# Second block: projections of x times the norm weight, with 1/rms applied to their products, and gate/up two slices ahead

## The chip, the cores and the metric

One core of one Trainium2 chip runs the whole program. The metric is the device time of one execution in microseconds; lower is better.

## What is computed

One sequence of 256 tokens with 1024 features passes two blocks. The first (two layers of a mixer with a state space scan, and a mixture of experts) isn't touched, but for the cut of one weight tile per layer. The second has four layers, each a mixer and an FFN, both behind an RMS norm:

```python
def rms_norm_2(x, g):
    y = xf * lax.rsqrt(jnp.mean(xf * xf, axis=-1, keepdims=True) + EPS)
    return (y * g.astype(F32)).astype(x.dtype)

def swiglu(h, w_gate_up, w_down):
    g, u = jnp.split(h @ w_gate_up, 2, axis=-1)
    return (jax.nn.silu(g) * u) @ w_down

for i in range(4):
    h = rms_norm_2(x, mix_norm_g[i])
    # i = 0, 3: forgetting_attention (q, k, v and 16 forget logits from h @ w_in)
    # i = 1: s5_layer (u = h @ w_in, scan, gelu, glu); i = 2: multiscale_pool
    x = x + mix
    x = x + swiglu(rms_norm_2(x, ffn_norm_g[i]), ffn_w_gate_up[i], ffn_w_down[i])
return rms_norm_2(x, final_norm_g)
```

The norm's factor 1/rms belongs to a token, so it commutes with a projection over features.

## The kernel before

x stands in SBUF with features on partitions, as 8 chunks of 128 features by 256 tokens. Every matmul of a projection is made of three (`mm3`, L655): weight and activation are both split into a rounded "high" part and the rest, "low", and high by high, high by low, low by high are added up in PSUM. Weights come as tiles of 1024 features by 256 columns (1 MB) into a ring of four (`ring`), loaded by SP's queue once `tile_free` says that the tile four before was used. For tile t ACT writes high (`make_high`, L1204, 128x2048 elements) into one of two buffers, so only after tile t-2 is free; then DVE and POOL each subtract one half for low (`make_low`, L362), and PE waits for both in `low_ready` (L353). The down weights of the FFN go the same way in tiles of 128 by 1024 (`make_down_high` L1214, `make_down_low` L373), with `down_free` in place of `tile_free`; down high (d) waits until d-2 was used. Each engine works through its own program in order.

A norm goes: ACT squares x by pairs of chunks (`squares`, L1239), PE sums them over partitions with 8 matmuls against 1/1024 (`mean_square`, L694), ACT takes the root (`root`, L1245), DVE the reciprocal and then, by chunk, x * gain / rms (`scale`, L1615), ACT its high part (`split_high`, L1249), DVE its low (L1626). PE starts a projection when chunk 0 is there and waits for each further one (`ready`).

A projection (`project`, L703) is a list of groups of 24 matmuls, two groups per weight tile, that write to PSUM banks in turn; an eviction frees a bank. In fox (layers 0 and 3, PE L1006, ACT L1469, DVE L2047) the forget logits come first in a tile of their own (`foxf`), then 24 groups of `foxin` (8 of V, 8 of Q, 8 of K, all evicted by ACT), then attention over 16 heads, then 8 groups of `foxout`, whose results DVE adds to x (`residual`, L1838). s5 (layer 1) has 8 groups of `s5in`, a scan loop, and 16 of `glu`. Layer 2 pools on DVE and needs the whole normed h.

An FFN has 22 slices of 128 hidden features (PE L964, ACT L1450, DVE L2011, POOL L502). `gate_up(j)` is 48 matmuls into bank 4 + j % 2 (gate in one half, up in the other), `down(j)` 24 into banks 0 to 3, which collect all slices. The order on PE is gate_up(j+1), down(j). Written out, the order of the other engines for slice j is

```python
# ACT: wait tile_free; silu(gate) -> gact; make_high(tile j+2); make_down_high(j+1)
# DVE: wait gact; hraw = gact * up (PSUM); hid high; hid low; make_low(tile j+2); make_down_low(j+1)
# POOL: make_low(tile j+2); make_down_low(j+1)
```

where tile j+2 for the last two slices is the first or second of the next stage. In FFN 0 DVE also computes the s5 matrices behind slices 1 to 3 (`s5_matrices`, L2139). After down(21) DVE adds the banks to x (`add_sum`, L2033).

## Time and profile before

| what | value |
|---|---|
| runs | 2779.86, 2789.84, 2791.86 us |
| median | 2789.84 us |
| profiled execution: span | 2783.9 us |
| profiled execution: own time beside the span | none given by the page |
| mean granted TensorE clock | 0.894 of full |
| PE / PEld busy | 2328.6 / 1960.5 us (84% / 70%) |
| DVE / ACT / POOL busy | 1625.2 / 1104.4 / 1323.9 us (58% / 40% / 48%) |
| second block | from about 1290 us to the end |

A row of a timeline gives start and length in us, engine, line, operation and what it writes and reads; in square brackets the idle time before and the engine and line that ended it. PE is the matmul stream, PEld its weight loads. The tiles have the program's names: `high` and `ring_halves` are a weight's high and low, `dhigh` and `dring_halves` the down weight's, `ssdb_halves` and `HT_halves` the activation's, `border` the hidden slice, `bank` PSUM, `wide` holds the squares.

### The profile page before, as it was taken

Reading aid. Unit: us, or ns where it says so; the run is one execution under the profiler, and the core shown is the slowest. Engines: PE = TensorE matmul, PEld = TensorE weight load, DVE = VectorE, ACT = ScalarE, POOL = GpSimd, SP = SyncE. Lnnn points to the kernel's source line nnn. Section 1 sums busy time; section 2 is a strip of 40 time slices with the busy share of each in tenths; the row PEclk is TensorE's granted clock in tenths of the full one; section 3 lists DMA queues with packets and bytes.
Section 4 is the critical chain, followed back from the end, with each engine's and each line's share of the span. In section 5 each row is a group of like instructions: output and inputs, shape, how many; then the busy total and the mean of one; then the engine's idle time right before and its main releaser. Section 6 shows DMA issues by size and latency. Waiting matters only on the chain.

```text
span 2783.9 us, 41385 instructions
## 1 busy us (share of the span) xinstructions
PE 2328.6 (84%) x15250; PEld 1960.5 (70%) x15250; DVE 1625.2 (58%) x2522; ACT 1104.4 (40%) x1581; POOL 1323.9 (48%) x744
## 2 busy tenths in 40 slices
PE   5998777788498767785999997768999799999998
PEld 2864545677385466674868995325899699887998
DVE  3488464477558545674247555996555755523654
ACT  3222533466433435764434442001443344444443
POOL 2320132588442336882654552874565256441553
PEclk7995888899797888997989998668999899999999
DMA  5258602699326037883405441001455244342442
GB/s 228 91 202 322 217 15 91 228 341 344 144 96 252 1 112 268 321 296 133 171 24 199 186 172 71 0 0 52 165 192 189 91 181 182 135 152 91 152 181 91
DMA packets 93047, 443.73 MB, mean 159 GB/s; under 512 B 9088, under 2 KB 25600, under 8 KB 56704
## 3 DMA queue, kind: packets, MB, share of 16 engines
q1 hardware_dynamic: 79104, 390.10, 38.6%
q0 software_dynamic: 8496, 31.99, 3.0%
q10 hardware_dynamic: 5328, 20.04, 1.8%
q8 instruction: 77, 1.26, 0.2%
q14 instruction: 42, 0.34, 0.0%
HBM read 401.20 MB, written 40.89 MB: 159 GB/s over the span
## 4 chain that ended last, share of the span: by engine, by line
PE 40%; DVE 5%; POOL 3%; ACT 2%; DVEq 2%; POOLq 1%; issue 1%; DMA 0%; ACTq 0%
PE bank L657 11%; PE bank L658 11%; PE bank L659 11%; POOL ring_halves L371 2%; PE bank L699 2%; ACT high L1212 1%; PE bank L1123 1%; POOLq L593 1%; DVEq L2179 1%; PE bank L1061 1%; DVE HT L1633 1%; POOLq L598 1%; PE bank L1038 1%; DVE rstd L1618 1%; PE bank L1051 1%
## 5 line engine op out<-in xcount | busy, mean ns | idle before, releaser
L371 POOL TENSOR_TENSOR ring_halves<-ring,high 128x1024 fp32r<-128x1024 f32 (+1 forms) x230 | 814.2, 3541 | 953.9 <-ACT high L1212 953.9
L657 PE MATMUL bank<-ssdb_halves,high 128*128 128x256 f32 (+1 forms) x2080 | 619.6, 298 | 65.8 <-DVE HT_halves L1627 34.8
L658 PE MATMUL bank<-HT_halves,high 128*128 128x256 f32 (+1 forms) x2096 | 627.4, 299 | 0.0
L659 PE MATMUL bank<-ssdb_halves,ring_halves 128*128 128x256 f32 (+1 forms) x2080 | 615.5, 296 | 0.0
L1212 ACT CAST high<-ring 128x2048 fp32r<-128x2048 f32 x230 | 438.0, 1906 | 89.7 <-PE bank L659 89.7
L657 PEld LDWEIGHTS bank<-ssdb_halves,high 128*128 128x128 f32 x2080 | 400.8, 193 | 90.5 <-issue 61.2
L371 DVE TENSOR_TENSOR ring_halves<-ring,high 128x1024 fp32r<-128x1024 f32 x200 | 279.5, 1398 | 248.0 <-ACT high L1212 247.9
L658 PEld LDWEIGHTS bank<-HT_halves,high 128*128 128x128 f32 x2096 | 402.6, 192 | 8.9
L659 PEld LDWEIGHTS bank<-ssdb_halves,ring_halves 128*128 128x128 f32 x2080 | 398.4, 192 | 9.6
L378 DVE TENSOR_TENSOR dring_halves<-dring,dhigh 128x512 fp32r<-128x512 f32 x152 | 309.6, 2037 | 53.1 <-ACT dhigh L1218 53.0
L378 POOL TENSOR_TENSOR dring_halves<-dring,dhigh 128x512 fp32r<-128x512 f32 x152 | 264.5, 1740 | 80.7 <-ACT dhigh L1218 80.6
L657 PE MATMUL bank<-border_halves,dhigh 128*128 128x256 f32 x704 | 197.5, 281 | 0.0
L659 PE MATMUL bank<-border_halves,dring_halves 128*128 128x256 f32 x704 | 197.3, 280 | 0.0
L658 PE MATMUL bank<-border_halves,dhigh 128*128 128x256 f32 x704 | 197.3, 280 | 0.0
L1218 ACT CAST dhigh<-dring 128x1024 fp32r<-128x1024 f32 x152 | 160.8, 1058 | 54.2 <-PE bank L659 54.1
L659 PE MATMUL bank<-high,HT_halves 128*128 128x256 f32 x640 | 182.0, 284 | 0.0
L1456 ACT ACTIVATE border<-bank 128x256 f32<-128x256 f32 x88 | 33.8, 384 | 365.0 <-PE bank L659 365.0
L657 PE MATMUL bank<-high,HT_halves 128*128 128x256 f32 x512 | 156.8, 306 | 18.0 <-POOL ring_halves L371 11.0
L2017 DVE TENSOR_TENSOR border<-border,bank 128x256 f32<-128x256 f32 x88 | 37.1, 422 | 213.9 <-ACT border L1456 213.1
L1123 PE MATMUL bank<-wide,zs_b 128*32 128x256 f32 x256 | 96.7, 547 | 62.5 <-DVE wide L2190 62.5
L658 PE MATMUL bank<-ring_halves,HT_halves 128*128 128x256 f32 x512 | 145.5, 284 | 0.0
L657 PEld LDWEIGHTS bank<-border_halves,dhigh 128*128 128x128 f32 x704 | 132.6, 188 | 0.1
(415 smaller groups left out, 4603.3 us busy)
## 6 DMA issues: line engine op xcount, KB each, us to landing
ring<-in_ffn SPq DMA_DIRECT2D x88, 1024.0 KB, 5.4
ring<-in_moe SPq DMA_DIRECT2D x64, 1024.0 KB, 7.3
ring<-in_ada SPq DMA_DIRECT2D x48, 1024.0 KB, 6.9
dring<-in_ffn_down SPq DMA_DIRECT2D x88, 512.0 KB, 3.6
dring<-in_moe_down SPq DMA_DIRECT2D x64, 512.0 KB, 4.6
ring<-in_foxin SPq DMA_DIRECT2D x24, 1024.0 KB, 4.8
ring<-in_win SPq DMA_DIRECT2D x22, 1024.0 KB, 4.8
zs_b<-x_slots POOLq DMA_DIRECT2D x32, 512.0 KB, 8.8
```

The costliest lines, as they stand in the source:

```text
L371: eng.tensor_tensor(low, w, h, ALU.subtract).then_inc(sem(f"low_{engine}"), 1)
L378: eng.tensor_tensor(low, w, h, ALU.subtract).then_inc(sem(f"down_low_{engine}"), 1)
L593: pool.drain()
L657: mm(o, a[0], b[0], start=first, stop=last and bool(kw), **kw)
L658: mm(o, a[0], b[1], start=False, stop=last and bool(kw), **kw)
L659: return mm(o, a[1], b[0], start=False, stop=last, **kw)
L699: i = mm(ps[7][:, 0:tok.stop - tok.start], k("mean1024"), sq[:, c, tok], start=c == 0, stop=c == KC - 1)
L1123: i = mm(y, cT[:, part, j, :], z, start=False, stop=n == 3, skip_group_check=True, tile_position=(0, q))
L1212: nc.scalar.copy(r(high[c % HIGH][:]), ring[t % RING][:]).then_inc(sem("high"), 1)
L1218: nc.scalar.copy(r(dhigh[d % HIGH][:]), dring[d % RING][:]).then_inc(sem("down_high"), 1)
L1456: act_fn(gact[:, j % 2, :], ps[4 + j % 2][:, 0:T], ACT.Silu).then_inc(sem("gate_act"), 1)
L2017: tt(hraw, gact[:, j % 2, :], ps[4 + j % 2][:, T:2 * T], ALU.mult)
```

## The change

For every projection of the second block behind a norm (all but pooling), ACT now writes the high part of x * gain straight from x, chunk by chunk as x gets ready (`x_high`), and the squares with it; DVE writes the low part (`x_low`), called from inside the loops that add to x. DVE adds the squares of the 8 chunks up (`square_sum`), so that PE's mean is one matmul (`sum_squares`), placed behind the first groups; root and reciprocal follow (`inv_root`). 1/rms then multiplies the products: DVE evicts Q, K and s5's u with it, ACT V with a column of it that PE turns, DVE the forget logits; in the FFN DVE multiplies gate and up by it from PSUM into `gu` (SBUF), which silu and the product read. The first groups run side by side, chunk by chunk (`first`, `gate_up_first`). In the FFN PE's order is gate_up(j+2), down(j). Forget logits' softplus moves behind group 12. Weight tiles outside the FFNs and experts are cut at three quarters for DVE, one for POOL. `F2r` is a second place for the low part, so that x_low can write while foxout and glu still read `H2r`.

The core of the diff:

```diff
+            CUT.append(0 if _n[0] not in WITH_DVE else TILE // 2 if _n[0] in IN_SLICES else 3 * TILE // 4)
...
-            cut = TILE // 2 if shared(c) else 0
+            cut = CUT[c]
...
+            def sum_squares(n):
+
+                pe.wait_ge(*at("row_stats", ("sum", n)))
+                mm(ps[7][:, 0:T], k("mean1024"), sq[:, 0, 0:T], start=True, stop=True).then_inc(*done("mean_square", n))
...
+                if first is not None:
+                    heads = [(n, j, lag, out_ap(ps[bank]), pairs(*low_ready(SPLIT_AT[n]))) for n, j, bank, lag, (out_ap, pairs) in first]
+                    for step in range(KC + max(h[2] for h in heads)):
+                        if step < KC:
+                            pe.wait_ge(*ready(step))
+                        for n, j, lag, o, pairs in heads:
+                            if 0 <= step - lag < KC:
+                                i = mm3(o, *next(pairs), step == lag, step - lag == KC - 1)
+                                if step - lag == KC - 1:
+                                    group_done(n, j, i)
+                    start = 1 + max(j for n, j, *_ in first if n == name)
...
+                    if j >= 2 or not isinstance(g, int):
+                        pe.wait_ge(sem("gu_scaled"), gu0 + j - 1 + RING * g)
...
+                def gate_up_first():
+
+                    wh, wl = low_ready(c0)
+                    for c in range(KC):
+                        pe.wait_ge(*ready(c))
+                        for m in range(2):
+                            a = slice(c * TCOLS + m * P, c * TCOLS + m * P + P)
+                            i = mm3(ps[4][:, m * T:m * T + T], (wh[:, a], wl[:, a]), (r(xh(c)), r(xl(c))),
+                                    c == 0 and m == 0, c == KC - 1, skip_group_check=True)
...
-                gate_up(0, 0, ready)
-                turns = (slices - 1) // RING
+                gate_up_first()
+                for b in range(4):
+                    mm(ps[b][:], zeros[:, 0:P], zeros, start=True, stop=True)
+                sum_squares(mean)
+                gate_up(1, 0)
+                turns = (slices - 2) // RING
                 with pe.Fori(0, turns) as g:
                     for j in range(RING):
-                        gate_up(j + 1, g)
+                        gate_up(j + 2, g)
                         down(j, g)
                 for j in range(turns * RING, slices):
-                    if j + 1 < slices:
-                        gate_up(j + 1, 0)
+                    if j + 2 < slices:
+                        gate_up(j + 2, 0)
                     down(j, 0)
...
+                def after(j):
+                    if j == 2:
+                        sum_squares(name)
+                    if j == 3:
+                        pe.wait_ge(*at("row_stats", ("rstd", name)))
+                        for b in range(TB):
+                            i = mm(ps[7][:, 300 + b:301 + b], rstd[0:1, b * P:b * P + P], one[0:1, 0:1], start=True, stop=True)
+                        i.then_inc(*done("mean_square", ("col", i_layer)))
+                    if j == 6:
+                        narrow_turned(("foxf", i_layer), 16, 7, 256, TB).then_inc(*done("f_raw", i_layer))
...
+                        [(("foxf", i_layer), 0, 5, 0, forget), (("foxin", i_layer), 0, 0, 0, groups[0])], after)
...
+                        lambda j: at("u_sb", j), [(("s5in", 1), j, j, 2 * j, groups[j]) for j in range(2)],
+                        lambda j: sum_squares(("s5",)) if j == 2 else None)
...
+            def x_high(n, c, gain, ready):
+
+                act.wait_ge(*ready(c))
+                act_fn(r(H2h[:, c, :]), XT2[:, c, :], ACT.Identity, scale=gain[:, c:c + 1]).then_inc(*done("norm_high", (n, c)))
+                if c % 2:
+                    act_fn(sq[:, c - 1:c + 1, 0:T], XT[:, c - 1:c + 1, 0:T], ACT.Square).then_inc(*done("squares", (n, c // 2)))
...
+            def swiglu(name, slices, n):
+                c0, d0, gu0 = SPLIT_AT[name], DOWN_AT[name], base("gu_scaled", name)
                 loop_base("gate_act", name, slices)

                 def one(j, g):
-                    act.wait_ge(sem("tile_free"), t0 + j + 1 + RING * g)
-                    act_fn(gact[:, j % 2, :], ps[4 + j % 2][:, 0:T], ACT.Silu).then_inc(sem("gate_act"), 1)
+                    act.wait_ge(sem("gu_scaled"), gu0 + j + 1 + RING * g)
+                    act_fn(gact[:, j % 2, :], gu[:, 0], ACT.Silu).then_inc(sem("gate_act"), 1)
                     make_high(c0 + j + 2, g)
                     if j + 1 < slices:
                         make_down_high(d0 + j + 1, g)

                 make_down_high(d0)
+                root(n, slice(0, T))
                 slices_loop(act, slices, one, 1 if d0 == 0 else 0)
...
+                root(("fox", i_layer), slice(0, T))
+                act.wait_ge(*at("row_stats", ("col", i_layer)))
+                for j in range(8):
                     act.wait_ge(*proj_at(("foxin", i_layer), j))
-                    bank = ps[j % 4]
-                    if j < 8:
-                        i = nc.scalar.copy(vtok[:, j % 2, TCOLS * (j // 2):TCOLS * (j // 2) + TCOLS], bank[:, 0:TCOLS])
-                    elif j < 16:
-                        i = nc.scalar.mul(Q2[:, j - 8, :], bank[:, 0:T], HD ** -0.5)
-                    else:
-                        i = nc.scalar.copy(K2[:, j - 16, :], bank[:, 0:T])
-                    i.then_inc(*done("fox_sb", (i_layer, j)))
+                    act_fn(vtok[:, j % 2, TCOLS * (j // 2):TCOLS * (j // 2) + TCOLS], ps[j % 4][:, 0:TCOLS], ACT.Identity,
+                           scale=r_col[:, j % 2:j % 2 + 1]).then_inc(*done("v_sb", (i_layer, j)))
                     tiles_after(("foxin", i_layer), j)
+                for j in range(9, 24, 2):
+                    tiles_after(("foxin", i_layer), j)
+                    if j == 11:
+                        softplus_log("f", i_layer, fx[:, 3, :, :], fx[:, 1, :, :])
...
+                root(("s5",), slice(0, T))
+                for j in range(1, KC, 2):
                     tiles_after(("s5in", 1), j)
...
                 for c in range(KC):
@@ -1527,6 +1584,9 @@
                         act.wait_ge(*at("res_dve", (("glu", 1), j - 2)))
                     act_fn(sig[:, j % 2, 0:T], ps[4 + (2 * j + 1) % 4][:, 0:T], ACT.Sigmoid).then_inc(*done("glu_gate", j))
                     tiles_after(("glu", 1), 2 * j + 1)
+                    if j:
+                        x_next(j - 1)
+                x_next(KC - 1)

             ada(0)
             root(("mix", 0), slice(0, 2 * T))
@@ -1564,21 +1624,27 @@
                 make_high(SPLIT_AT["foxf", 0] + a)
             for i_layer in range(4):
                 name = (("fox", 0), ("s5",), ("pool",), ("fox", 3))[i_layer]
-                squares(name, slice(0, T), lambda c: at("x_ready", (("ffn", i_layer - 1), c) if i_layer else ("first", c)))
-                root(name, slice(0, T))
-                if i_layer != 2:
-                    split_high(name, H2h, H2, None, 1)
+                x_ready = lambda c: at("x_ready", (("ffn", i_layer - 1), c) if i_layer else ("first", c))
+                if i_layer == 2:
+                    squares(name, slice(0, T), x_ready)
+                    root(name, slice(0, T))
+                else:
+                    for c in range(KC):
+                        x_high(name, c, v(f"mix_g{i_layer}"), x_ready)
                 last_res = (("foxout", 0), ("glu", 1), ("poolw", 2), ("foxout", 3))[i_layer]
+                x_next = lambda c: x_high(("ffn2", i_layer), c, v(f"ffn_g{i_layer}"), lambda c: at("res_dve", (last_res, c)))
                 if i_layer in (0, 3):
                     fox(i_layer)
-                    for a in range(HALF_D):
-                        tiles_after(last_res, 2 * a + 1)
+                    for c in range(KC):
+                        if c % 2:
+                            tiles_after(last_res, c)
+                        x_next(c)
...
+            def x_low(n, c, gain, to):
+
+                dve.wait_ge(*at("norm_high", (n, c)))
+                stt(r(to[:, c, :]), XT2[:, c, :], gain[:, c:c + 1], H2h[:, c, :], ALU.mult, ALU.subtract)\
+                    .then_inc(*done("normed", (n, c)))
+
+            def square_sum(n):
+
+                dve.wait_ge(*at("squares", (n, KC // 2 - 1)))
+                for a in (4, 2, 1):
+                    i = tt(sq[:, 0:a, 0:T], sq[:, 0:a, 0:T], sq[:, a:2 * a, 0:T], ALU.add)
+                    if a > 1:
+                        dve.drain()
+                i.then_inc(*done("row_stats", ("sum", n)))
+
+            def inv_root(n):
+
+                dve.wait_ge(*at("root", n))
+                nc.vector.reciprocal(rstd[:, 0:T], rms[:, 0:T]).then_inc(*done("row_stats", ("rstd", n)))
...
+                    if then is not None and j:
+                        then(j - 1)
+                    if then is not None and j == KC - 1:
+                        then(j)
                     if j % 2:
                         tiles(name, j // 2)
...
                 def one(j, g):
+                    dve.wait_ge(sem("tile_free"), t0 + j + 1 + RING * g)
+                    tt(gu, ps[4 + j % 2][:].rearrange("p (a b) -> p a b", a=2), rstd[:, 0:T].unsqueeze(1).to_broadcast([P, 2, T]),
+                       ALU.mult).then_inc(sem("gu_scaled"), 1)
+                    if c0 + j + 2 < len(SPLIT):
+                        make_low(dve, "dve", c0 + j + 2, g)
                     dve.wait_ge(sem("gate_act"), act0 + j + 1 + RING * g)
-                    tt(hraw, gact[:, j % 2, :], ps[4 + j % 2][:, T:2 * T], ALU.mult)
+                    tt(hraw, gact[:, j % 2, :], gu[:, 1], ALU.mult)
                     dve.drain()
+                    dve.wait_ge(sem("down_free"), d0 + j - 1 + RING * g)
                     nc.vector.tensor_copy(r(hid[:, j % 2, 0, :]), hraw)
                     dve.drain()
                     tt(r(hid[:, j % 2, 1, :]), hraw, hid[:, j % 2, 0, :], ALU.subtract).then_inc(sem("hidden"), 1)
-                    if c0 + j + 2 < len(SPLIT):
-                        make_low(dve, "dve", c0 + j + 2, g)
                     if j + 1 < slices:
                         make_down_low(dve, "dve", d0 + j + 1, g)
                     if between is not None and isinstance(g, int) and 1 <= j < RING:
                         between(j - 1)
                     dve.drain()

+                square_sum(n)
                 make_down_low(dve, "dve", d0)
+                inv_root(n)
...
+            def fox(i_layer, then):
+                name = ("foxin", i_layer)
+                square_sum(("fox", i_layer))
+                tiles(("foxf", i_layer))
+                inv_root(("fox", i_layer))
+                dve.wait_ge(*proj_at(("foxf", i_layer), 0))
+                tt(narrow_sb[0:16, 0:T], ps[5][0:16, 0:T], rstd[0:16, 0:T], ALU.mult).then_inc(*done("narrow_sb", ("foxf", i_layer)))
+                dve.wait_ge(*at("mean_square", ("col", i_layer)))
+                nc.vector.tensor_copy(r_col, ps[7][:, 300:300 + TB]).then_inc(*done("row_stats", ("col", i_layer)))
+                for j in range(24):
+                    if j >= 8:
+                        dve.wait_ge(*proj_at(name, j))
+                        if j < 16:
+                            i = stt(Q2[:, j - 8, :], ps[j % 4][:, 0:T], HD ** -0.5, rstd[:, 0:T], ALU.mult, ALU.mult)
+                        else:
+                            i = tt(K2[:, j - 16, :], ps[j % 4][:, 0:T], rstd[:, 0:T], ALU.mult)
+                        i.then_inc(*done("row_stats", ("qk", i_layer, j)))
+                    if j % 2:
+                        tiles(name, j // 2)
+                    if j == 12:
+                        forget(i_layer)
+                attend(i_layer)
+                residual(("foxout", i_layer), [0, 1, 2, 3], then=then)
...
+                square_sum(("s5",))
+                inv_root(("s5",))
+                for j in range(KC):
+                    dve.wait_ge(*proj_at(("s5in", 1), j))
+                    tt(Q2[:, j, :], ps[j % 4][:, 0:T], rstd[:, 0:T], ALU.mult).then_inc(*done("u_sb", j))
+                    if j % 2:
+                        tiles(("s5in", 1), j // 2)
```

## Rows read from the trace of the kernel before

**Rows 1.** The page: its first line, and the chain by engine.

```profile
span 2783.9 us, 41385 instructions
...
PE 40%; DVE 5%; POOL 3%; ACT 2%; DVEq 2%; POOLq 1%; issue 1%; DMA 0%; ACTq 0%
```

**Rows 2.** Windows, inside FFN 0: us; PE, PEld, DVE, ACT, POOL busy; clock; DMA.

```profile
1500.00:1670.00 170.00, 170.00 (x1443) 169.86 (x1441) 106.51 (x114) 69.92 (x65) 98.47 (x40) 1.00 0.49 181
```

**Rows 3.** Joints after fox 0 and FFN 0: chain in time; ACT timeline; one window.

```profile
1472.03 1.90 ACT high L1212
1474.51 5.42 PE bank L699 x16
...
1674.43 0.64 ACT wide L1242
...
1679.38 1.75 DVE rstd L1618
...
1500.80 1.05 ACT L1218 CAST dhigh<-dring 128x1024 fp32r<-128x1024 f32 x1 [0.66 <-PE bank L659]
...
1485.40:1488.80 3.40, 3.40 (x15) 3.12 (x15) 3.08 (x9) 2.26 (x5) 0.00 (x0) 0.51 0.02 5
```

**Rows 4.** Timelines of ACT, DVE, POOL, one FFN slice: start, us, operation [idle before].

```profile
1549.13 0.38 ACT L1456 ACTIVATE border<-bank 128x256 f32<-128x256 f32 x1 [4.60 <-PE bank L659]
1549.41 1.90 ACT L1212 CAST high<-ring 128x2048 fp32r<-128x2048 f32 x1
...
1549.55 0.42 DVE L2017 TENSOR_TENSOR border<-border,bank 128x256 f32<-128x256 f32 x1 [2.63 <-ACT border L1456]
...
1550.41 0.42 DVE L2021 TENSOR_TENSOR border_halves<-border,border_halves 128x256 fp32r<-128x256 f32 x1
1551.35 1.22 DVE L371 TENSOR_TENSOR ring_halves<-ring,high 128x1024 fp32r<-128x1024 f32 x1 [0.51 <-ACT high L1212]
1553.07 2.30 DVE L378 TENSOR_TENSOR dring_halves<-dring,dhigh 128x512 fp32r<-128x512 f32 x1 [0.49 <-ACT dhigh L1218]
...
1551.39 3.43 POOL L371 TENSOR_TENSOR ring_halves<-ring,high 128x1024 fp32r<-128x1024 f32 x1 [3.33 <-ACT high L1212]
```

**Rows 5.** One line's instructions over the run: ns min/median/max.

```profile
L371 POOL TENSOR_TENSOR ring_halves<-ring,high x230: 2354/3431/4852, 49.6 to 2748.3; 128x1024 fp32r<-128x1024 f32 x99, 128x2048 fp32r<-128x2048 f32 x16
...
L378 DVE TENSOR_TENSOR dring_halves<-dring,dhigh x152: 679/2306/2879, 503.1 to 2758.5; 128x512 fp32r<-128x512 f32 x152
...
L2017 DVE TENSOR_TENSOR border<-border,bank x88: 420/422/423, 1492.7 to 2763.4; 128x256 f32<-128x256 f32 x88
...
L2021 DVE TENSOR_TENSOR border_halves<-border,border_halves x88: 424/425/1356, 1493.6 to 2764.3; 128x256 fp32r<-128x256 f32 x88
...
L2176 DVE TENSOR_TENSOR wide<-bank,XT x16: 676/678/692, 1717.4 to 1891.1; 128x512 f32<-128x512 f32 x16
```

**Rows 6.** Timelines of fox 0's input projection: POOL, PE, ACT.

```profile
1322.36 3.40 POOL L371 TENSOR_TENSOR ring_halves<-ring,high 128x1024 fp32r<-128x1024 f32 x1 [4.65 <-ACT high L1212]
...
1325.90 0.36 PE L657 MATMUL bank<-high,ssdb_halves 128*128 128x256 f32 x1 [1.33 <-POOL ring_halves L371]
...
1331.83 0.37 ACT L1477 COPY zs_b<-bank 128x256 f32<-128x256 f32 x1 [2.45 <-PE bank L659]
...
1337.76 1.91 ACT L1212 CAST high<-ring 128x2048 fp32r<-128x2048 f32 x1
...
1349.53 1.89 ACT L1212 CAST high<-ring 128x2048 fp32r<-128x2048 f32 x1
```

**Rows 7.** DVE timeline, first and last of six products for s5 in FFN 0.

```profile
1505.31 0.68 DVE L2153 TENSOR_TENSOR wide<-MIX,s5p 128x512 f32<-128x512 f32 x1
...
1508.48 0.69 DVE L2159 TENSOR_TENSOR MIX<-wide 128x512 f32<-128x512 f32 x1
```

**Rows 8.** ACT timeline: end of s5's input projection; fox 3's group 5.

```profile
1708.77 1.90 ACT L1212 CAST high<-ring 128x2048 fp32r<-128x2048 f32 x1
...
2436.50 0.37 ACT L1477 COPY zs_b<-bank 128x256 f32<-128x256 f32 x1 [2.46 <-PE bank L659]
```

130 lines of the change are left out of this document (70 added, 60 removed).

## The prediction

> **What bounds the kernel now.** I read the chain that ended last first: TensorE stands in it with 40% of the span, other engines with little [rows 1]. The busy time by stretch says where that holds: in a stretch of 170 us inside the first FFN, PE is busy for all of it, 1443 matmuls, so 0.1178 us each, at the full clock [rows 2]; the other three FFNs read the same. There G(j), the 48 matmuls of gate/up of slice j, takes 5.65 us, D(j), the 24 of down, 2.83, a slice 8.48, and 22 slices 187 us. Nothing the change does can shorten that. What it can shorten are the joints. At the joint fox 0 to FFN 0 the last projection ends just before 1472.03; then squares, mean (5.42 on PE), root, reciprocal (1.75, the same at every joint) and scaling go one after the other, and D(0) ends only at 1500.80 [rows 3]: E + 28.8 us, E being the last projection's end, of which G(0), G(1), D(0) need 14.1. There is slack of 14.7 us. The seven changed joints have some of this kind.
>
> **One slice of the FFN before** [rows 4]. G ends, ACT's silu starts 1549.13 and the next weight tile's high half 0.28 later (1.90); DVE makes the hidden slice in three operations (0.42 the first, the last, 0.42, begins 0.86 after it: 1.28 together), then its part of low (1.22); POOL its part (3.43, from 1551.39). When D(j-1) ends, ACT makes the down tile's high (1.05 [rows 3]), then DVE (from 1553.07) and POOL its low. DVE's 2.30 for 512 elements, against 0.68 at least, and POOL's 3431 ns against 2354 [rows 5], are waits for each other: DVE goes first, POOL follows, DVE comes third. Alone, 1024 elements cost POOL about 2.25, 512 about 1.2.
>
> **The change in the FFN loop.** PE now runs G(j+2), D(j). ACT still makes down high (j+1) before it looks at slice j+1, and that high waits for D(j-1), which now ends 8.5 us later than before against G(j+1). So a serial chain starts at T, the end of D(j-1): down high T+0.04 to 1.09; DVE down low from 1.12, 0.68; drain; the new scaling of both halves out of PSUM, 512 elements, 0.68 by an s5 operation of that form [rows 5], from 1.87 to 2.55; silu from 2.59, high (j+3) from 2.87 to 4.78; DVE low 4.82 to 6.05; POOL low from 4.86, 3.43, to 8.30; PE starts 0.14 later, 8.44 (at 1325.90 it started so much after the end of the POOL low from 1322.36, [rows 6]). PE would want G(j+3) at 8.32. The chain spans two slices, so a slice takes (8.44+0.16+8.48)/2 = 8.54. The same kind of chain for projection tiles comes to 11.67 per two tiles where the rows show 11.77 between 1337.76 and 1349.53 [rows 6]; I take 8.57. Loss 0.09 x 80 slices = **7 us**. The bounds are 0 and 32 (below).
>
> DVE has a ring of its own, one slice long: down low, scaling (u+0.75 to 1.43), silu, high (to 3.66), its low, then `gact*gu`. What ends the wait before that product? Its second operand was in PSUM and is now in SBUF. Row: the old product with a PSUM operand took 420 to 423 ns in all 88 cases, the subtraction next to it with both in SBUF 424 to 1356 [rows 5]; so I let the new one wait for POOL's low (7.18), and the ring is 8.40 us long, 0.08 under PE's 8.48. The Trainium skill, SBUF — State Buffer, section Who interferes with whom, has it as a rule: a DVE instruction with two SBUF inputs blocks against a GpSimd one that reads SBUF, and the later waits for the whole instruction. By that rule the sum stays as it is; without it the ring would be 6.3 and the forecast 6 to 9 us lower. The trace agrees.
>
> **End of each FFN.** After G(21) there are three D's, D(19), D(20), D(21). With T the end of D(19): DVE can scale slice 21 only after down low 21 (T+1.12), and high and lows of the next stage's tile stand before its product: high to T+4.78, DVE's three quarters 1.83 (1.22 x 1.5) to 6.65, POOL's quarter 1.2 to 7.85, the three hidden operations to about T+9.0 (9.4 where the next tile is cut in halves), while PE wants it at T+2.67. Before, it followed G(21) by 2 us under a D of 2.83. Stall 6.5, 6.9, 6.5 and, where no tile follows, 1.7 (counting 0.8 before D(20)): **21.5 us**. Bounds 15 (no blocking by POOL) and 25.
>
> **s5 matrices.** In FFN 0 DVE computes six products between slices, 3.9 us from 1505.31 to the end of 1508.48's row [rows 7], twice, and once one of 0.7. DVE had over 4 us of slack per slice; in the new ring it has none. With the wait for POOL's down low (1.1) 5.0 each: **10.7 us**. Bounds 5 and 14 (the second took 7.2 beside POOL).
>
> **Start of each FFN.** Chunks 0 to 5 are ready under the last projections, so G(0) starts at E. ACT makes a weight high (1.9) before x_high of chunk 7, and POOL's low then holds DVE's x_low back to about E+4.7; PE comes to chunk 7 at E+4.9. Covered, with no slack. G(0) E+5.65, four zeroing matmuls 6.7. The square sum (1.22+0.68+0.42, drains) starts behind x_low 7 and a tile low at 6.0, with down low 0 of POOL between: sum on PE at 9.1. G(1) 9.6 to 15.3. Root 10.0, reciprocal 1.75, scaling 12.55, silu, high (2) 14.8 (it was free from 5.7 on, but ACT is in order), POOL 18.3; G(2) 18.4 to 24.1; D(0) 26.9. Against 28.8, with one G more done: 28.8-26.9+5.65 = 7.5. I take it for the joints after fox 0, s5's glu and fox 3, and 6.2 after pooling (DVE's add loop gets eight x_low of 0.42, partly in its slack): **28.7 us**. Bounds 22 and 36.
>
> **Projections.** s5in: FFN 0's last D ends near 1673.6, 0.8 before the first square [rows 3]. Chunks come at about 0.8 us (add 0.42, x_low 0.42); both head groups are done 8.1 us after the FFN; a wait of 2.7 follows before group 4 (root before high, then DVE low 1.83 of three quarters). Group 7 ends near 1701.9 against 1708.77, when ACT takes the tile up [rows 8], and the diagonal after it waits 0.5 less for POOL: **7.3 us**. Fox: heads are done 10 to 11 us sooner, but the tile after waits for the low (2.3), and ACT cannot take V 0 and 1 before sum, root, reciprocal and column (about 12 us after the heads); high (foxin 2) stands behind that, and PE waits 5.9 before group 4. Group 5 ends at 1329.1 against 1331.8 in fox 0 and 2432.6 against 2436.5 in fox 3 [rows 6, 8]: 2.6 and 3.9. Tiles after that no longer wait for POOL (1.91 + 1.83 + 1.2 = 5.0 under 5.65): 0.23 x 9, less 1.35 where the softplus holds ACT at group 11, 0.75 each, and 1.0 each in foxout. **10.0 us**. In glu x_high behind high, and x_low behind POOL, take the gain back: 0. The pooling norm stays. Bounds of all projections 8 and 24. The rt tile's new cut is a single tile beside routing: 0.
>
> **Clock.** After a joint's gaps PE ran 3.4 us at half speed (granted 0.51, the 1.2 GHz level) [rows 3], 1.7 us lost each time PE had work. The joints' dips are inside the E+28.8. New holes of 3 to 6 us: three FFN ends, four at G(2) and four at the sum, two by the matrices, two in fox, one in s5. With a dip in about half, **12 us**; bounds 0 and 20. A hole of 1.33 us [rows 6] brought none.
>
> **Sum**: -28.7 -7.3 -10.0 +7 +21.5 +10.7 +12 = +5. The page gives the profiled execution's span, 2783.9, and no time of its own beside it; the three runs have their median 5.9 above that, their fastest 4.0 below. Span 2789; median **2795 us**. No change, if anything slower: what the joints give, the FFNs take. A measurement tells 0.5% (14 us) from no change.
>
> **Rivals.**
> *Joints win* (faster): the loop stays on PE (8.48), holes bring few dips, the product isn't blocked. -46 +15 +8.5 +4 = -18.5: 2771. For it: the steady loss is 0.1 us in 8.5, and PE is at 100% today. Against: the end-of-FFN hole follows from the order of the queues alone.
> *DVE's ring decides* (slower): one ring in which down low, scaling, silu, high, both lows and three hidden operations follow each other. At 8.40 it hides; from 8.68 on it alone makes the kernel slower by 0.5%. Beside POOL the hidden operations took up to 1356 ns instead of 424 [rows 5]; one such a slice gives up to 0.93. At 8.9, 0.42 x 80 = 34 instead of 7: 2822. Against: POOL is idle while they run.
> *It doesn't do what it says*: G(0) starts early and then waits for chunks 6 and 7, because ACT's high and POOL's low stand before them. One POOL low more (2.3) and its hop, at four joints, is 10: 2806.
>
> **Chances.** Forecast 0.42; joints win 0.23; ring 0.25; late chunks 0.10. Faster 0.23, same 0.42, slower 0.35. All bounds together give 2750 to 2851; for 8 in 10 I take 2768 to 2824, from just under the first rival to just above the second; the forecast's own range is 2781 to 2804.
>
> **What would show it.** PE idle in the FFN loops of 0.1 us a slice before G, released by POOL's low; a hole of about 6 us before D(21), released by DVE's hidden; 5 us twice in FFN 0; G(0) starting within 0.2 us of E; PE waiting 2 to 3 us at the sum and 3 at G(2); about 6 us before fox group 4. I am wrong if the hole before D(21) is missing, or if PE idles over 0.3 us in a plain slice.

## The result, and the profile after

The changed kernel takes 2857.4 us (median of 2848.4, 2854.9, 2859.8 and 2865.0) beside 2787.1 for the kernel before on the same chip: ratio 1.0244, 95% interval 1.0213 to 1.0275. That is slower, and above the range. The profiled execution of after has a span of 2846.7 us against 2783.9 [rows 1]. The page of after, its first line and the chain by engine:

```profile
span 2846.7 us, 41465 instructions
...
PE 18%; issue 9%; DVEq 9%; DVE 8%; POOL 6%; ACT 5%; POOLq 1%; DMA 0%; ACTq 0%
```

TensorE's share of the chain fell from 40% to 18%: other engines now set the end of slices. Where, the windows of after show, beside [rows 2]:

```profile
core 0: us, PE busy (x) PEld busy (x) DVE busy (x) ACT busy (x) POOL busy (x), PEclk, DMA share, GB/s
1560.00:1590.00 30.00, 29.99 (x252) 29.55 (x251) 20.22 (x23) 12.75 (x13) 17.73 (x8) 1.00 0.50 185
2050.00:2180.00 130.00, 119.71 (x986) 116.89 (x986) 93.14 (x83) 47.94 (x45) 64.54 (x28) 1.00 0.46 176
2290.00:2430.00 140.00, 129.60 (x1069) 126.78 (x1069) 99.40 (x90) 52.09 (x48) 68.68 (x30) 1.00 0.47 176
```

Early in FFN 0 PE is still full. From 1589 on, and in the other three FFNs almost from the start, it idles 7 to 8% at the full clock. The starts of silu give the slices: 8.49 us before; in after 8.5 to 8.8 in FFN 0 from 1520 (behind the s5 matrices) until 1580, one of 9.0, then mostly 9.3 to 9.9. Two of these slices in the timelines of DVE, POOL and ACT (start, us, operation, idle before), to be read beside [rows 4]:

```profile
1626.69 0.69 DVE L2109 TENSOR_TENSOR wide<-bank,rstd 128x512 f32<-128x512 f32 x1 [0.45 <-issue]
1629.67 1.23 DVE L376 TENSOR_TENSOR ring_halves<-ring,high 128x1024 fp32r<-128x1024 f32 x1 [2.28 <-ACT high L1264]
1630.81 2.60 DVE L2114 TENSOR_TENSOR border<-border,wide 128x256 f32<-128x256 f32 x1
1633.56 1.39 DVE L2117 CAST border_halves<-border 128x256 fp32r<-128x256 f32 x1 [0.15 <-issue]
1635.03 0.43 DVE L2119 TENSOR_TENSOR border_halves<-border,border_halves 128x256 fp32r<-128x256 f32 x1
1635.38 0.68 DVE L383 TENSOR_TENSOR dring_halves<-dring,dhigh 128x512 fp32r<-128x512 f32 x1
1636.22 0.69 DVE L2109 TENSOR_TENSOR wide<-bank,rstd 128x512 f32<-128x512 f32 x1 [0.17 <-issue]
...
1643.10 0.29 DVE L2117 CAST border_halves<-border 128x256 fp32r<-128x256 f32 x1
1643.47 1.36 DVE L2119 TENSOR_TENSOR border_halves<-border,border_halves 128x256 fp32r<-128x256 f32 x1
...
1629.71 3.42 POOL L376 TENSOR_TENSOR ring_halves<-ring,high 128x1024 fp32r<-128x1024 f32 x1 [4.35 <-ACT high L1264]
1633.52 1.29 POOL L383 TENSOR_TENSOR dring_halves<-dring,dhigh 128x512 fp32r<-128x512 f32 x1 [0.39 <-ACT dhigh L1270]
...
1643.18 1.36 POOL L383 TENSOR_TENSOR dring_halves<-dring,dhigh 128x512 fp32r<-128x512 f32 x1 [0.52 <-ACT dhigh L1270]
...
1632.40 1.04 ACT L1270 CAST dhigh<-dring 128x1024 fp32r<-128x1024 f32 x1 [2.77 <-PE bank L664]
```

The product (L2114) waits for POOL's weight low and takes 2.60 instead of 0.42. It ends at 1633.41, and at 1633.44 ACT's down high is ready: POOL, which has waited 0.39 us for it, starts its half of the down low 0.04 us before DVE's cast, and the cast takes 1.39 instead of 0.29. In the next slice the cast gets through, and the subtraction is the one caught (1.36). Down low, scaling and silu come a microsecond later, and so does the next product. Of the 88 slices 16 have the cast caught in this way and 45 the subtraction. The same three lines over the whole run (ns min/median/max):

```profile
L2114 DVE TENSOR_TENSOR border<-border,wide x88: 425/2611/2628, 1477.7 to 2827.0; 128x256 f32<-128x256 f32 x88
...
L2117 DVE CAST border_halves<-border x88: 293/295/1424, 1480.4 to 2827.5; 128x256 fp32r<-128x256 f32 x88
...
L2119 DVE TENSOR_TENSOR border_halves<-border,border_halves x88: 424/1342/1556, 1481.7 to 2827.9; 128x256 fp32r<-128x256 f32 x88
```

TensorE's holes outside plain slices, in order: the sum at FFN 0's start, G(2) of FFN 1, two beside the s5 matrices, the two before D(20) and D(21) of FFN 0, and fox 0's wait before group 4 (the sum waited 1.68 in FFN 1 and 2.73 in FFN 3):

```profile
1469.98 1.22 PE L711 MATMUL bank<-wide,con 128*128 128x256 f32 x2 [3.71 <-DVE wide L1716]
...
1995.66 0.57 PE L662 MATMUL bank<-ssdb_halves,high 128*128 128x256 f32 x1 [3.43 <-POOL ring_halves L376]
...
1502.47 0.38 PE L662 MATMUL bank<-ssdb_halves,high 128*128 128x256 f32 x1 [4.35 <-POOL ring_halves L376]
1515.42 0.38 PE L662 MATMUL bank<-ssdb_halves,high 128*128 128x256 f32 x1 [2.66 <-POOL ring_halves L376]
...
1671.65 0.36 PE L662 MATMUL bank<-border_halves,dhigh 128*128 128x256 f32 x1 [1.31 <-DVE border_halves L2119]
1679.44 0.55 PE L662 MATMUL bank<-border_halves,dhigh 128*128 128x256 f32 x1 [4.71 <-DVE border_halves L2119]
...
1321.86 0.55 PE L662 MATMUL bank<-high,ssdb_halves 128*128 128x256 f32 x1 [5.92 <-POOL ring_halves L376]
```

### The profile page after: what moved, and what is told of

It is laid out like the page before. It is cut to its first block, busy times and chain, and to the rows that moved or that the text cites. A ratio compares the mean times of both kernels' runs of the same rounds, so it can differ in the third digit from the quotient of the medians.

```text
span 2846.7 us, 41465 instructions
## 1 busy us (share of the span) xinstructions
PE 2318.1 (81%) x15160; PEld 1947.1 (68%) x15160; DVE 1825.7 (64%) x2619; ACT 1095.6 (38%) x1539; POOL 1262.4 (44%) x744
## 4 chain that ended last, share of the span: by engine, by line
PE 18%; issue 9%; DVEq 9%; DVE 8%; POOL 6%; ACT 5%; POOLq 1%; DMA 0%; ACTq 0%
PE bank L662 5%; PE bank L663 4%; PE bank L664 4%; DVEq L2115 4%; ACT high L1264 4%; POOL ring_halves L376 4%; DVEq L2124 2%; DVE ring_halves L376 2%; DVE wide L2109 1%; PE bank L1177 1%; POOL dring_halves L383 1%; DVEq L2310 1%; DVE border_halves L2117 1%; PE bank L1161 1%; PE bank L1114 1%
## 5 line engine op out<-in xcount | busy, mean ns | idle before, releaser
L376 POOL TENSOR_TENSOR ring_halves<-ring,high 128x1024 fp32r<-128x1024 f32 (+2 forms) x230 | 779.9, 3392 | 1051.4 <-ACT high L1264 1051.4
L376 DVE TENSOR_TENSOR ring_halves<-ring,high 128x1024 fp32r<-128x1024 f32 (+1 forms) x200 | 301.8, 1509 | 322.9 <-ACT high L1264 322.8
L383 POOL TENSOR_TENSOR dring_halves<-dring,dhigh 128x512 fp32r<-128x512 f32 x152 | 236.3, 1555 | 103.2 <-ACT dhigh L1270 103.2
L2114 DVE TENSOR_TENSOR border<-border,wide 128x256 f32<-128x256 f32 x88 | 220.7, 2508 | 1.0 <-ACT border L1515 1.0
L662 PE MATMUL bank<-border_halves,dhigh 128*128 128x256 f32 x704 | 201.1, 286 | 21.8 <-DVE border_halves L2119 21.8
L663 PE MATMUL bank<-border_halves,dhigh 128*128 128x256 f32 x704 | 200.1, 284 | 0.0
L383 DVE TENSOR_TENSOR dring_halves<-dring,dhigh 128x512 fp32r<-128x512 f32 x152 | 181.6, 1194 | 24.9 <-ACT dhigh L1270 24.6
L662 PEld LDWEIGHTS bank<-border_halves,dhigh 128*128 128x128 f32 x704 | 135.3, 192 | 23.0 <-issue 23.0
L663 PEld LDWEIGHTS bank<-border_halves,dhigh 128*128 128x128 f32 x704 | 135.7, 193 | 0.0
```

What stands on the lines that cost most here:

```text
L376: eng.tensor_tensor(low, w, h, ALU.subtract).then_inc(sem(f"low_{engine}"), 1)
L383: eng.tensor_tensor(low, w, h, ALU.subtract).then_inc(sem(f"down_low_{engine}"), 1)
L662: mm(o, a[0], b[0], start=first, stop=last and bool(kw), **kw)
L663: mm(o, a[0], b[1], start=False, stop=last and bool(kw), **kw)
L2114: tt(hraw, gact[:, j % 2, :], gu[:, 1], ALU.mult)
```

## The experiments

My theory after the result: DVE's ring (the second rival) decides, and it got its length from two things in the order of DVE's queue, the product that waits for POOL's weight low and the hidden operations that then fall together with POOL's down low. Rivals were the look-ahead of two itself, the scaling itself, and plain overload of DVE. "Slice" in this table is the time from silu(5) to silu(20) of FFN 2, divided by 15; ratios are to the kernel before, which was measured beside every kernel (medians 2781 to 2787). So a gap between two rows of the table can be told from the medians or from the ratios, and the two can differ by some us; where it matters, both are given.

| kernel | us | ratio (95%) | slice |
|---|---|---|---|
| before | 2781 to 2787 | 1 | 8.49 |
| after | 2857.4 | 1.0244 (1.0213 to 1.0275) | 9.49 |
| 1: hidden operations first | 2790.0 | 1.0024 (1.0001 to 1.0048) | 8.79 |
| 2: DVE makes 7/8 of down low | 2844.5 | 1.0226 (1.0198 to 1.0254) | 9.12 |
| 3: as 1, one slice ahead | 2747.0 | 0.9872 (0.9846 to 0.9897) | 8.49 |
| 4: before, two ahead | 2800.9 | 1.0050 (1.0025 to 1.0074) | 8.49 |
| 5: as after, up scaled in PSUM | 2852.2 | 1.0232 (1.0171 to 1.0292) | 9.09 |
| 6: as 1, down tile made a slice later | 2772.1 | 0.9963 (0.9937 to 0.9988) | 8.52 |
| 7: as after, one slice ahead | 2857.1 | 1.0278 (1.0223 to 1.0332) | 9.38 |
| 8: as 3, joints reordered | 2744.2 | 0.9851 (0.9799 to 0.9903) | 8.49 |
| 9: as 5, bank released early | 2813.0 | 1.0115 (1.0080 to 1.0150) | 8.78 |
| 10: as 8, s5 matrices spread | 2733.4 | 0.9839 (0.9807 to 0.9870) | 8.49 |
| 11: as 3, tiles cut in halves | 2756.9 | 0.9928 (0.9901 to 0.9956) | 8.49 |
| 12: as after, POOL waits | 2808.5 | 1.0117 (1.0070 to 1.0163) | 8.76 |

**1. The order of DVE's queue.** `make_low(dve, ..., c0 + j + 2, g)` moves from ahead of the product to behind the subtraction:

```diff
-                    if c0 + j + 2 < len(SPLIT):
-                        make_low(dve, "dve", c0 + j + 2, g)
                     dve.wait_ge(sem("gate_act"), act0 + j + 1 + RING * g)
...
+                    if c0 + j + 2 < len(SPLIT):
+                        make_low(dve, "dve", c0 + j + 2, g)
                     if j + 1 < slices:
                         make_down_low(dve, "dve", d0 + j + 1, g)
```

> The changed kernel with DVE's order in the FFN slice alone altered: product, cast and subtraction of the hidden slice come ahead of DVE's half of the weight tile's low; TensorE still runs two slices ahead. Theory R (DVE's ring decides: the product waits for POOL's weight low, then cast or subtraction meets POOL's down low, 1.36 to 1.44 us instead of 0.29 and 0.42, so a slice takes 9.45 us): the product now runs beside no POOL work, the regime of 9.45 us goes, slices take 8.5 to 8.65 us (what is left is the chain from the end of D(j-1) to G(j+3)), the hole before D(21) shrinks from 5 us to under 2, the product's mean falls from 2508 ns to under 700, and the time falls by some 60 to 75 us from 2857 to 2780 to 2800, ratio to the kernel before about 1.00. Rival L (it is two slices ahead and the serial chain of down high, down low, scaling, silu, high, low that costs it): slices stay above 9.2 us and the time stays within 10 us of 2857. Rival S (the scaling itself is too much work for DVE): likewise above 9 us a slice.

2790.0 us: theory R. The order of DVE's queue alone is worth 67 us by the medians, 61 by the ratios. The product in this kernel, and TensorE's waits for POOL (us, times, longest), 76.0 in 69 times in after:

```profile
L2112 DVE TENSOR_TENSOR border<-border,wide x88: 424/426/429, 1480.4 to 2768.8; 128x256 f32<-128x256 f32 x88
...
PE bank L662 <- POOL ring_halves L376: 40.3, 26, 5.9
```

The slices are 8.79, above the 8.5 to 8.65 that R expected: what was left is the chain over two slices, below.

**2. Less of the down low on POOL.** `at_` is cut at 7/8 instead of 1/2 in the FFNs.

> The changed kernel, but in the FFNs DVE makes seven eighths of a down tile's low and POOL one eighth (before: a half each). Theory R (the collision of POOL's down low with DVE's cast or subtraction is what lengthens the slice): POOL's part takes some 0.4 us and is done before the hidden operations, DVE's part grows by 0.4 us; the regime of 9.45 becomes one of 8.9 to 9.1 us, cast and subtraction read 0.29 and 0.42 us nearly always, and the time falls by 25 to 40 us from 2857. Rival W (DVE simply has too much work in a slice, whatever it meets): 0.4 us more work makes slices of 9.8 us or more, and the time rises by 25 to 35 us to about 2885.

More work for DVE made the kernel no slower (2844.5, where overload would give 2885), so rival W falls. The slices went to 9.12, just above R's 8.9 to 9.1, and the cast's maximum to 440 ns, as R has it; the time fell by 13 us and not by 25 or more. FFN 0 is part of why: from silu(3) to silu(20) it gained 0.2 us, the others 5.2 to 5.9 each, since in after half of its slices never had the collision, and here all have DVE's 0.4 us more. The rest of the shortfall isn't explained.

**3. One slice ahead.** With 1's order, and on PE:

```diff
-                gate_up(1, 0)
-                turns = (slices - 2) // RING
+                turns = (slices - 1) // RING
...
-                        gate_up(j + 2, g)
+                        gate_up(j + 1, g)
                         down(j, g)
```

> The changed kernel with DVE's order as in the first of these runs, and gate/up one slice ahead of down instead of two (as in the kernel before); projections on x, the early start of G(0), and the scaling by 1/rms stay. Theory R with the joints as I priced them: TensorE sets 8.48 us a slice, the holes at the FFN ends (6 us each) and most of the waits beside the s5 matrices are gone, and the joints keep their gain: 2740 to 2765, ratio to the kernel before 0.983 to 0.992. Rival S (the scaling in the slice costs by itself, silu can't start before it): slices above 8.6 us, and the time at or above 2785. Rival J (the joints gain nothing that lasts): 2780 to 2790.

2747.0 us, faster than both kernels by more than the intervals. So the scaling out of PSUM costs nothing by itself, and the joints do gain.

**4. Two slices ahead alone, in the kernel before.** `gate_up(j + 2)` with the waits that it needs.

> The kernel before with one part of the change alone: TensorE runs gate/up two slices ahead of down (with the waits that this needs: G(j+2) for the hidden slice j whose bank it takes, DVE's cast for the down that reads its buffer). 1/rms is still in x, silu reads PSUM. Theory R (looking ahead needs no time by itself; what costs is the ring of DVE's with the scaling in it): DVE's ring is shorter by the scaling and its product runs ahead of the lows; slices of 8.5 to 8.6 us, FFN-end holes of 1 to 2 us, time 2787 to 2800, ratio 1.000 to 1.005. Rival L (two ahead costs by itself, since ACT's high of the down tile now waits for a down 8.5 us later): slices of 9 us or more, time 2830 or more.

2800.9, slices of 8.49: as R says, the look-ahead costs no steady time. One slice of 15.8 us beside the s5 matrices stands for half of the 14 us. DVE's cast waits for POOL in this kernel too (655 ns at the median, 294 alone), and the slices don't grow: a wait of this kind costs something only where the ring has no slack for it.

**5. Up scaled in place in PSUM.** Is it the product's second SBUF operand? Besides the edit shown, PE waits for `hidden` in place of `gu_scaled` before it takes the bank again.

```diff
-                    tt(gu, ps[4 + j % 2][:].rearrange("p (a b) -> p a b", a=2), rstd[:, 0:T].unsqueeze(1).to_broadcast([P, 2, T]),
-                       ALU.mult).then_inc(sem("gu_scaled"), 1)
+                    up = ps[4 + j % 2][:, T:2 * T]
+                    tt(up, up, rstd[:, 0:T], ALU.mult)
+                    tt(gu[:, 0], ps[4 + j % 2][:, 0:T], rstd[:, 0:T], ALU.mult).then_inc(sem("gu_scaled"), 1)
...
-                    tt(hraw, gact[:, j % 2, :], gu[:, 1], ALU.mult)
+                    tt(hraw, gact[:, j % 2, :], up, ALU.mult)
```

> The changed kernel in its own order, but DVE scales the up half in place in PSUM and only the gate half goes to SBUF, so that the product gact*up has one operand in PSUM again (TensorE waits for the hidden slice before it takes the bank). Theory R1 (it is the product's two SBUF operands that make it wait for POOL's weight low, and so the three hidden operations slide into POOL's down low): the product takes 420 to 430 ns in all 88 cases instead of 2508 on average; the cast then waits for POOL's low instead, but the three are done 0.4 us sooner, before the next down low; slices of 8.6 to 8.8 us throughout, no regime of 9.4, time 2785 to 2810. Rival R2 (the order alone: any operation behind DVE's low is late, wherever its operands are): the cast takes over the whole wait and meets POOL's down low as before; slices 9.3 us or more, time 2840 to 2860.

Product and cast of this kernel:

```profile
L2115 DVE TENSOR_TENSOR border<-border,bank x88: 411/414/420, 1484.3 to 2830.1; 128x256 f32<-128x256 f32 x88
...
L2118 DVE CAST border_halves<-border x88: 294/1946/2011, 1484.8 to 2830.6; 128x256 fp32r<-128x256 f32 x88
```

The operand decides whether the product waits; but the cast, from SBUF to SBUF, then takes over the wait, and the time did not fall (2852.2). The slices are 9.09, between R1's and R2's. R2's prediction of the time held, yet for another reason: the chief wait in the trace was PE's for the hidden slice, 72.4 us in 47 times, which my edit had put in. So this run could not tell the two apart, and 9 was made.

**6. The down tile one slice later.** `make_down_high`, `make_down_low` of j instead of j+1, with 1's order.

> The first experiment's kernel (two ahead, hidden operations first) with one more change: in slice j ACT, DVE and POOL make the down tile j and not j+1, so nothing in a slice waits for the down that has just ended before it scales. Theory C (the 8.76 us a slice that were left are the serial chain end of D(j-1), down high, down low, scaling, silu, high, POOL's low, G(j+3), over two slices): slices of 8.48 to 8.50 us, no hole at the FFN ends, 0.28 x 80 = 22 us and 4 ends of 2 us off 2790, and some beside the s5 matrices: 2740 to 2765. Rival P (it is POOL's 5.2 us of lows and its waits for DVE in a slice): slices stay above 8.7 us, time within 8 us of 2790.

The slices are 8.52, near the 8.48 to 8.50 of theory C and far from P's: the 8.79 was the serial chain. The whole came to 2772.1 and not to 2765 or less. I had written "no hole at the FFN ends"; the trace has one of 3.04 before D(21) of FFN 1, released by DVE's own down low, now the last thing in the slice. And the hole at G(2) is there in each FFN (3.42 us in FFN 2), and none of the orders tried with two slices ahead removed it: nothing is left for PE to do while the third weight tile is made. With one ahead D(0) stands there, and in kernel 3 no wait over 0.9 us is left at G(2). The two holes of this kernel:

```profile
2153.04 0.58 PE L660 MATMUL bank<-border_halves,dhigh 128*128 128x256 f32 x1 [3.04 <-DVE dring_halves L383]
...
2210.59 0.38 PE L660 MATMUL bank<-ssdb_halves,high 128*128 128x256 f32 x1 [3.42 <-POOL ring_halves L376]
```

**7. One slice ahead, DVE's order left as changed.**

> The changed kernel with one part undone: gate/up one slice ahead of down, as before; DVE's order (weight low, then the hidden operations) is the changed kernel's own. Theory R (a ring of DVE, ACT and POOL: scaling, silu, high, POOL's low, product, cast or subtraction behind POOL's down low, down low; how far TensorE looks ahead does not enter): slices of 9.3 to 9.6 us again, time 2810 to 2840, only the holes at the FFN ends gone. Rival L (the two slices ahead are needed for the ring to arise, the order is harmless without them): slices of 8.48 us, 2745 to 2765 as in the run with one ahead and the other order.

2857.1, the time of after, with slices of 9.3 to 9.7. How far PE looks ahead does not matter while the order stands, which refutes rival L. My range for it was too low: here the down high no longer waits for a down, so POOL's down low follows its weight low at once and catches the cast in 82 of the 88 slices, from the first on.

**8. The joint's order.** ACT takes chunk 7 of x before the last tile's high, DVE the sum before its low.

> The version with one slice ahead and the hidden operations first, and the joints reordered: after fox 0, s5 and fox 3 ACT takes chunk 7 of x (and its squares) before the last weight tile's high, and DVE sums the squares before that tile's low. Theory J (at the joint TensorE's 3.7 us hole at the sum is this one high of 1.9 us and POOL's low of 2.4 us that stand before chunk 7 and the sum, plus the half-speed start after it): the mean follows G(0) without a hole of more than 0.5 us, G(1) starts 3.5 us sooner, no stretch at the 1.2 GHz level there; 3.5 to 6 us at each of three joints, time 2730 to 2738, ratio to the kernel before 0.979 to 0.984. Rival K (the tile that is now made later is what G(1) waits for next): no gain, 2745 to 2752.

2744.2, below K's range by 1 us and within the interval of 3: no gain that can be told. PE's hole of 3.71 at the sum is gone, and one before G(1) has come for it, as rival K says; DVE's sum meets the same POOL low (4.53 us for the three operations where they took 2.48 in 3), and its weight low stands behind it:

```profile
1472.76 4.53 DVE L1718 TENSOR_TENSOR wide<-wide 128x1024 f32<-128x1024 f32 x3
1477.21 3.27 DVE L376 TENSOR_TENSOR ring_halves<-ring,high 128x1024 fp32r<-128x1024 f32 x1
...
1480.73 0.36 PE L662 MATMUL bank<-ssdb_halves,high 128*128 128x256 f32 x1 [2.38 <-DVE ring_halves L376]
```

**9. Run 5 with the bank released by the product.** `then_inc` on the product; PE waits for that.

> As the run with the up half scaled in place in PSUM, but TensorE takes the bank again as soon as the product has read it, not when the hidden slice is done; in that run 72 us of TensorE's waits were for the hidden slice, a wait that my edit had added. DVE's own ring was 8.0 us there (down low to subtraction: 2345.51 to 2353.54), and no operation met POOL's down low. Theory R1 (the product's SBUF operand makes DVE's ring 0.43 us longer, and that is what tips it past TensorE's slice): slices of 8.7 to 8.8 us, set by the serial chain over two slices, time 2785 to 2805. Rival R2 (the cast behind it keeps the ring as long): slices of 9.0 us or more, 2830 or more.

Between the two: 2813.0, but with slices of 8.78, R1's. So the 0.43 us which the product's operand puts on the ring is enough to tip it over. What stays above R1's time are the FFN ends (19.1 us of waits for the subtraction in seven holes, 7.0 in run 1), since the cast still waits for POOL there.

**10. The s5 matrices one instruction a slice**, between subtraction and weight low.

> The version with the reordered joints, and the s5 matrices taken one DVE instruction a slice, between the hidden slice's subtraction and the weight tile's low (slices 1 to 14 of FFN 0), instead of in three lumps behind the down low of slices 1 to 3. Theory M (the lumps cost because each waits 1.1 us for POOL's down low and then holds the next scaling by 3.9 us; where DVE waits for ACT's high anyway, an instruction of 0.7 us costs TensorE nothing): no slice of 11.97 us any more, all at 8.5 or under, 7 us less and perhaps 1 to 2 of clock: 2733 to 2738, ratio to the kernel before 0.981 to 0.984. Rival: each instruction now delays DVE's low by 0.2 to 0.7 us and POOL's low behind it, and the slices grow to 8.7: no gain.

2733.4, the fastest. The slices of 11.97 are gone (8.51 at most), and so are the slices of 7.2 behind them, in which PE had caught up; from silu(0) to silu(20) of FFN 0 this kernel takes 6.0 us less than 8. Its interval overlaps that of 8, so the gain itself rests on the trace.

**11. Projection tiles cut in halves again**, on kernel 3.

> The version with one slice ahead and the hidden operations first, with DVE's share of a projection tile's low back at one half, as in the kernel before (the change had made it three quarters). Theory T (by the rows, DVE 1.83 and POOL 1.2 of a three-quarter cut end 0.4 us sooner than the two halves, and PE waits for the low at 0.2 us a tile in fox and 1.0 us in the tiles next to it): 3 to 10 us slower than 2747: 2750 to 2757. Rival (the lows are hidden under two groups of 5.65 us either way): within 2 us of 2747.

2756.9, 10 us more than 3, and 15 by the ratios, whose intervals just don't overlap (0.9901 against 0.9897): the new cut helps, by as much as T says or more. In fox 0's projection PE's waits for POOL's low rose from 8.5 us to 10.8, and the longest wait for x_low from 9.5 to 10.6.

**12. The collision alone taken away.**

```diff
                     if j + 1 < slices:
+                        pool.wait_ge(sem("hidden"), hid0 + j + 1 + RING * g)
                         make_down_low(pool, "pool", d0 + j + 1, g)
```

> The changed kernel with one wait added and nothing else: in an FFN slice POOL starts its half of the down low only when the hidden slice is done, so it can't meet DVE's cast or subtraction. Theory R (after the collision's 1.1 us nothing but the serial chain is left, which gave 8.76 us a slice): the cast and the subtraction read 0.29 and 0.42 us, the product still waits 2.5 us, slices of 8.6 to 8.8 us, time 2790 to 2810. Rival Q (the collision is a symptom: the ring with the blocked product is over 9 us by itself, or POOL's later down low makes a new wait): slices of 9.2 us or more, time above 2835.

One wait more, and 49 us less by the medians, 35 by the ratios: 2808.5. The cast and the subtraction of this kernel, to be read beside L2117 and L2119 of after:

```profile
L2118 DVE CAST border_halves<-border x88: 293/294/297, 1485.5 to 2788.3; 128x256 fp32r<-128x256 f32 x88
...
L2120 DVE TENSOR_TENSOR border_halves<-border,border_halves x88: 424/426/428, 1485.9 to 2788.7; 128x256 fp32r<-128x256 f32 x88
```

The product still waits here (2515 ns on average). From silu(3) to silu(20) the four FFNs together are 42.6 us shorter than in after. So of the loss of 70 us more than half, some 43 with 35 and 49 as bounds, is the collision, and 1, 3 and 6 say what most of the rest is: late hidden slices at the FFN ends, and the chain.

## Why the prediction was wrong

**The step that failed** is DVE's ring in the FFN loop. I had it at 8.40 us, 0.08 under PE, and set against the second rival that "POOL is idle while they run". The rival had the ring and the kind of loss right: it named up to 1356 ns from [rows 5], and a caught cast or subtraction took 1.14 to 1.56 us. Its price was too low: it let a slice grow by 0.42 and gave 2822 us, where the slices grew by 1.0. And POOL was idle there only on paper. My own working had POOL's weight low end at T+8.30 and the next down high ready at about T'+1.09, T' being T plus a slice: 9.6. The hidden operations then run to T+9.5 (in after the subtraction ends 1.16 after POOL's weight low, 1578.69 against 1577.53). A tenth of a microsecond was all that kept them apart, and I had not worked this margin out. Once one slice slips (in FFN 0 the first long period is that from 1580.4, 9.02 us, at a turn of the loop where ACT also loads a table, 1.28 us), the collision makes each ring longer than PE's slice, and the FFN doesn't get back to 8.5. In the period after it POOL's half of the down low starts 0.13 us before DVE's own half, and this is the first operation caught since the s5 matrices, 1.78 instead of 0.69; one period later it is the subtraction:

```profile
1595.93 0.43 DVE L2119 TENSOR_TENSOR border_halves<-border,border_halves 128x256 fp32r<-128x256 f32 x1
1596.27 1.78 DVE L383 TENSOR_TENSOR dring_halves<-dring,dhigh 128x512 fp32r<-128x512 f32 x1
...
1605.45 1.35 DVE L2119 TENSOR_TENSOR border_halves<-border,border_halves 128x256 fp32r<-128x256 f32 x1
...
1596.14 1.36 POOL L383 TENSOR_TENSOR dring_halves<-dring,dhigh 128x512 fp32r<-128x512 f32 x1 [1.02 <-ACT dhigh L1270]
```

Run 12 shows what the collision costs by taking it alone away. That the table load made the first slip is only seen in its place, not shown: the load at 1552.6 lay in a slice of 8.8, and slices of 8.6 and 8.7 followed.

**Loop, predicted +7.** From silu(3) to silu(20) the four FFNs lost 11.0, 17.0, 16.9 and 16.6 us against before: 62. The term was also too low without the collision: the chain over two slices is 8.76 to 8.79 (runs 1, 9, 12), not 8.57, since down high starts 0.2 after the last row of a down and not 0.04, and each fourth slice has the table load on it (in FFN 1 and 2 of run 12 every second slice is long, 8.9 and 9.3 in turn). That alone would be some 0.2 x 80 = 16 us.

**FFN ends, predicted 21.5.** All waits for the subtraction together are 21.8 us in seven holes, 6.0 and 8.1 in FFN 0 and 1: right, and from the queues' order as argued.

**s5 matrices, predicted 10.7.** Holes of 4.35 and 2.66; the slices are 13.17 and 12.93 where 9.45 is the rule, 7.2 us. Right in kind, 3 too much.

**Start of each FFN.** G(0) starts without a wait for x at the fox 0 joint; in FFN 1 it waits 0.45, in FFN 3 for nothing over 0.3; so "it doesn't do what it says" falls. The hole at the sum is 3.71 in FFN 0 and smaller in the others, at G(2) 1.27 in FFN 0 and 3.42 or 3.43 in the others; I had 2 to 3 and 3.

**Projections.** Fox 0's waits are 1.87 and 5.92 where I had 2.3 and 5.9; s5's 2.56 where I had 2.7.

**Joints, projections and clock together, predicted -46 + 12 = -34.** Kernel 3 against before is -39 with 6 us of matrices in it (from silu(0) to silu(20) FFN 0 takes 171.3, FFN 1 165.3), so -45; the change has the four holes at G(2) besides, 11.5 us. That leaves -34. The whole agrees, the clock in it doesn't: TensorE's busy time times the missing share of the granted clock, added up over windows of 2 us from 1290 on, is 6 us more in after than in before outside the two attentions and the s5 layer, where I had 12, and 6 more in the s5 layer, which I had not counted. How the rest is shared between the starts of the FFNs and the projections wasn't measured.

**The sum**: -34 +62 +22 +7 = 57, against 63 between the two profiled executions and 70 between medians. That it comes near 63 is luck: in the profile of after the two attention stretches were 12.9 us shorter than in that of before (9.9 in fox 0, see the last section, 3.0 in fox 3), with the same code in them. Outside them and the FFN loops after took 14.2 us more, where the terms make -5. So 13 us by the medians and 19 by the profiles are not assigned.

## What to carry to other kernels

An engine's ring that fits under the bound by a tenth of a microsecond isn't hidden: work out the margin of every pair of operations that may not run together, and ask what a slip of one does to the next round. Put what another engine waits for ahead of bulk work in a queue; here that order alone was 61 to 67 us. A deeper look-ahead pays only if it fills a hole: here one slice ahead with the hidden operations first (2747.0), joints reordered and matrices spread (2733.4, 1.6% under the kernel before), beats two ahead in any form tried.

## What the runs showed of the hardware

A cast of 128x256 from SBUF to SBUF waits for POOL's subtraction as the product with two SBUF operands does (294 ns alone, 1946 at the median in run 5), while the product with one operand in PSUM never did (411 to 423 in all kernels that have it). Whoever starts first holds the other off to its end: the cast of 1633.56 ended at 1634.95, behind a POOL subtraction that had started 0.04 us before it and ended at 1634.81. By the Trainium skill, SBUF — State Buffer, section Who interferes with whom, that is an exclusive lock on the interface shared by both engines, which a cast can take too. The trace agrees.

The attention of fox 0, the same code in all kernels, took from 46.5 to 56.4 us in their profiles. From the first to the last of its 16 maxima over the keys, before, after and in kernel 3 (the clock is the number after POOL):

```profile
1388.09:1444.52 56.43, 50.80 (x225) 32.60 (x223) 27.00 (x76) 22.41 (x86) 35.54 (x69) 0.82 0.01 5
...
1385.86:1432.36 46.50, 41.77 (x224) 27.20 (x223) 25.92 (x76) 22.25 (x86) 34.58 (x69) 1.00 0.01 3
...
1382.65:1432.05 49.40, 44.80 (x224) 29.23 (x223) 26.35 (x77) 22.26 (x86) 34.48 (x69) 0.93 0.01 3
```

Its matmuls are the same (224 or 225 records), and parts of it ran at the 1.2 GHz level in some profiles and not in others (from 1390 to 1402 the granted clock is 0.50 in before and 1.00 in after): 10 us of difference between two profiles that no edit explains. Among kernels with an identical fox 0 up to there it was 0.93 (kernel 3) and 0.81 (kernel 8). Each kernel has one profile, so whether it goes by the kernel or by the execution isn't shown. Whoever compares two profiles of such a program should take this stretch out first.
